# The experts' gelu written out with ScalarE's tanh, in a two-block model on one core

## The reference

```python
idx = ...
gate = jax.nn.softmax(best_s, axis=-1)
u = jnp.take(down, idx, axis=0)
act = jax.nn.gelu(jnp.einsum('thkd,td->thk', u, xb))
v = jnp.take(up, idx, axis=0)
return jnp.einsum('thk,thkd->td', (gate * act).astype(v.dtype), v)
```

## Time and profile before

| | |
|---|---|
| median of 3 runs | 3067.49 us (3066.1 to 3071.52) |
| the profiled execution | 3067.7 us |
| its span in the trace | 3065.5 us |
| layer 0 rows (first DMA issue to last diagonal) | 1703 to 2353 us |
| layer 1 rows | 2400 to 3053 us |
| busy over the span: PE, DVE, ACT, POOL | 88%, 69%, 43%, 19% |
| bytes moved by the row gathers | 536.9 MB |

### The profile page before, as it was taken

How to read it: one execution, slowest core, us unless ns; L and a number is a source line. 1 busy time by engine, 2 the same in 40 slices (tenths; PEclk the granted TensorE clock), 3 DMA queues, 4 the chain that set the end, 5 groups by cost and what they waited for, 6 DMA issues and landing times. The chain is left out here.

```text
span 3065.5 us, 45483 instructions
## 1 busy us (share of the span) xinstructions
PE 2693.6 (88%) x16982; PEld 1808.3 (59%) x16982; DVE 2114.3 (69%) x3898; ACT 1317.5 (43%) x2949; POOL 579.6 (19%) x516
## 2 busy tenths in 40 slices
PE   8999977999999987899989998877777899777777
PEld 6887776788788777778876653322223654223232
DVE  7756776775876677577555777777764777777764
ACT  5443444543544442454344344444443344444443
POOL 0000000000000000000000354444441244444442
PEclk9999999999999999899999999999999999999999
DMA  9855201785875510268643799999998699999997
GB/s 323 282 184 173 89 4 69 251 306 219 295 262 191 185 52 4 98 245 307 240 187 119 306 427 427 427 427 427 427 427 355 258 427 426 427 427 427 427 427 305
DMA packets 256748, 864.65 MB, mean 282 GB/s; under 512 B 15504, under 2 KB 139280, under 8 KB 183952
## 3 DMA queue, kind: packets, MB, share of 16 engines
q0 software_dynamic: 73728, 536.90, 41.6%
q1 hardware_dynamic: 182800, 324.85, 30.1%
HBM read 853.04 MB, written 8.65 MB: 281 GB/s over the span
## 5 line engine op out<-in xcount | busy, mean ns | idle before, releaser
L3634 POOL DMA_INDIRECT raw_weights<-peer_rows,expert_ids x208 | 232.2, 1116 | 2053.6 <-DVE expert_ids L152 1771.8
L3744 PE MATMUL banks<-raw_weights,diagonals 128*128 128x512 f32 x832 | 395.1, 615 | 92.2 <-ACT diagonals L185 92.2
L486 PE MATMUL banks<-weight_parts_hi,normedT_hi 128*128 128x512 f32 (+2 forms) x1152 | 452.8, 393 | 16.9 <-DVE weight_parts_lo L1662 5.4
L487 PE MATMUL banks<-weight_parts_lo,normedT_hi 128*128 128x512 f32 (+2 forms) x1152 | 441.4, 383 | 0.0
L488 PE MATMUL banks<-weight_parts_hi,normedT_lo 128*128 128x512 f32 (+2 forms) x1152 | 441.4, 383 | 0.0
L3744 PE MATMUL banks<-query_weights,diagonals 128*128 128x512 f32 x704 | 333.7, 611 | 70.1 <-ACT diagonals L185 69.6
L161 DVE CUSTOM_DVE_ANT_0 modulation<-raw_weights,normed 128x1024 f32<-128x1024 f32 x208 | 255.3, 1228 | 140.9 <-DMA raw_weights<-peer_rows,expert_ids 130.3
L3744 PEld LDWEIGHTS banks<-raw_weights,diagonals 128*128 128x128 f32 x832 | 151.7, 193 | 326.6 <-ACT diagonals L185 187.6
L185 ACT ACTIVATE gelu<-dots 128x1 f32<-128x1 f32 x512 | 102.3, 200 | 498.9 <-DVE dots L161 498.1
L3744 PE MATMUL banks<-modulation,diagonals 128*128 128x512 f32 x512 | 248.8, 622 | 63.8 <-ACT diagonals L185 63.7
L161 DVE CUSTOM_DVE_ANT_0 modulation<-query_weights,normed 128x1024 f32<-128x1024 f32 x176 | 216.0, 1227 | 113.2 <-DMA query_weights<-peer_rows,expert_ids 103.3
(11 more groups left out here) (407 smaller groups left out, 4495.3 us busy)
## 6 DMA issues: line engine op xcount, KB each, us to landing
raw_weights<-ffn_in SPq DMA_DIRECT2D x88, 1024.0 KB, 7.6
side_weights<-mod_tiles SPq DMA_DIRECT2D x48, 1024.0 KB, 5.9
raw_weights<-ffn_out SPq DMA_DIRECT2D x44, 1024.0 KB, 6.7
raw_weights<-w_in SPq DMA_DIRECT2D x28, 1024.0 KB, 5.0
query_weights<-peer_w_q SPq DMA_DIRECT2D x16, 1024.0 KB, 10.7
raw_weights<-w_in SPq DMA_DIRECT2D x10, 1536.0 KB, 6.5
raw_weights<-w_branch SPq DMA_DIRECT2D x8, 1024.0 KB, 7.3
raw_weights<-w_out SPq DMA_DIRECT2D x8, 1024.0 KB, 5.1
```

The source lines that it names most:

```text
L486: nc.tensor.matmul(out, lhs.hi, rhs.hi, start=start, stop=False)
L487: nc.tensor.matmul(out, lhs.hi, rhs.lo, start=False, stop=False)
L3634: nc.gpsimd.indirect_dma_start(out=ring.rows(g), out_offset=None, in_=table, in_offset=bass.IndirectOffsetOnAxis(ap=ids[:, n, t:t + 1], ax ...
L3744: last = nc.tensor.matmul(k.bank(2 * j + half), diag[:, g % DIAGS, :], ring.rows(g)[:, D + half * BANK:D + (half + 1) * BANK], start=t == ...
```

## The change

The gelu function of ScalarE is replaced by its formula. With x the dot product and w the gate weight halved, ScalarE computes x², w·x, GELU_CUBE·x² + GELU_ROOT, the tanh of that times x, and (tanh)·(w·x) + (w·x). The half is moved into `gate` on VectorE, as the second operation of an instruction that is there already. The first two copies are marked free, so they wait for no drain; the other three and the diagonal come after a drain each.

```diff
+GELU_ROOT = math.sqrt(2.0 / math.pi)
+GELU_CUBE = 0.044715 * GELU_ROOT
...
                 def gate(n):
                     dve.wait_ge(S["gate_exped"], n + 1)
                     o.recip(tot[:, n:n + 1], tot[:, n:n + 1])
-                    o.ts(best[:, n], best[:, n], tot[:, n:n + 1], ALU.mult).then_inc(S["gates_ready"], 1)
+                    o.ts(best[:, n], best[:, n], tot[:, n:n + 1], ALU.mult, 0.5, ALU.mult).then_inc(S["gates_ready"], 1)
...
                         act.wait_ge(S["dotted"], g + 1)
-                        o.fn(gelu[:, g:g + 1], dots[:, g:g + 1], ACT.Gelu_apprx_tanh, free=True)
-                        o.fn(coef[:, g:g + 1], gelu[:, g:g + 1], ACT.Copy, scale=best[:, n, t:t + 1])
+                        x = dots[:, g:g + 1]
+                        o.fn(gelu[:, g:g + 1], x, ACT.Copy, scale=x, free=True)
+                        o.fn(coef[:, g:g + 1], x, ACT.Copy, scale=best[:, n, t:t + 1], free=True)
+                        o.fn(gelu[:, g:g + 1], gelu[:, g:g + 1], ACT.Copy, scale=GELU_CUBE, bias=GELU_ROOT)
+                        o.fn(gelu[:, g:g + 1], gelu[:, g:g + 1], ACT.Tanh, scale=x)
+                        o.fn(gelu[:, g:g + 1], gelu[:, g:g + 1], ACT.Identity, scale=coef[:, g:g + 1], bias=coef[:, g:g + 1])
                         if g >= DIAGS:
 
                             act.wait_ge(S["prod"], g - DIAGS + 1)
-                        o.fn(diag[:, g % DIAGS, :], C("ident"), ACT.Copy, scale=coef[:, g:g + 1]).then_inc(S["grown"], 1)
+                        o.fn(diag[:, g % DIAGS, :], C("ident"), ACT.Copy, scale=gelu[:, g:g + 1]).then_inc(S["grown"], 1)
```

## The result

The changed kernel takes 3078.46 us (median of 6 runs, 3076.93 to 3086.31) against 3067.55 us for the kernel before (6 runs, 3066.1 to 3071.52). The ratio is 1.0034, with a 95% interval of 1.0019 to 1.0049: slower by 10.9 us. The profiled execution took 3077.13 us, its span 3075.0. Lines are numbered 2 higher behind the new constants (L187 is the helper of the earlier trace rows, L3750 the matmul of the earlier trace rows).

A forecast was written before the change was run, and what follows sets the result against it. DMA gathers bound the steady rows; in the rounds the longer ScalarE chain runs their queue dry. Idle DMA 1.1 to 2.6 and 0 to 1.4, ends 2.0, upper values plus 1: +7.0 us, 3074.5; range 3068.0 to 3088.0.

The forecast's parts named there:

- ScalarE's row: ScalarE per row: 1.63 us to the diagonal, 1.94 row to row, 1.01 longer than before; not the bound of steady rows.
- The loads: Two 1.28 us table loads around each `weigh` on ScalarE: taken as gone if Exp and Tanh share a table set.
- the loads stay: Rival: Tanh lies in another table set than Exp, so loads around each `weigh` remain; about +22 us, 3089.5; chance 0.10.
- The queue covers it: Rival: with a ScalarE step under about 1.88 us, gather-queue slack covers the rounds; only +2.0 us, 3069.7; chance 0.36.
- Faster, by the loads: Rival: removed loads, some 77 us of ScalarE, show as a gain; judged no gain (+1.7 us); chance 0.04 for faster.
- The round: From restart to restart at each layer's start: 17.82 us in place of 16.03, 18.15 with a `weigh`, against 17.19 of DMA.
- and the last takes 1.72: Term for the last of a round's seven rows on TensorE: 1.72 us, in the sum 2.35 + 9.70 + 1.72 = 13.77.
- The first burst: Layer 0's first seven rows, paced by ScalarE: 13.4 us against 12.0, less 0.27, so the first restart 1.1 late.
- The slack: Lateness the gather queue absorbs after the rounds: 6.0 to 7.5 us in layer 1, 8.2 to 9.7 in layer 0.
- If 7.0 is what a busy queue needs: Gather latency in a short queue, 7.0 us instead of the idle 5.5; layer 1's DMA idle time then 2.6, not 1.1.
- The ends: Last row of each layer, its chain exposed from landing to norm: 1.01 us longer each, 2.0 us in all.

The follow-up runs named there:

- e7: Changed kernel with the old gelu function in tanh's place, rest of the row unchanged, so the table loads stay: 3106.87 us, ratio 1.0121.
- e1: Changed kernel with ScalarE's copies of queriesT and key_scores two rows later, so three diagonals are ready at a restart: 3072.03 us, ratio 1.0015.
- e4: Kernel before with Tanh in place of the gelu function, rest of the formula left out: 3064.02 us, ratio 0.9986.
- e8: Kernel before with a spare gelu behind `weigh(0)`, loading its table ahead of the first row, and `weigh(1)` behind row 4: 3064.29 us, ratio 0.9994.
- e3: Changed kernel with the formula only in groups 4 to 15 of each layer, the gelu function in the others: 3070.12 us, ratio 1.0007.
- e2: Changed kernel with the formula only in groups 0 to 3 of each layer (64 rows), the old form in the others: 3072.51 us, ratio 1.0017.

## Why the prediction was right

The forecast was slower, 3074.5 us, +7.0 on the profiled execution; measured was +10.9, 3078.46, inside the range. The mechanism is the one that it named, a queue that runs short in the rounds and two exposed ends; its sizes were too small, and one loss of 1.6 us wasn't foreseen.

- **ScalarE's row: as predicted.** 1.93 from row to row and 1.63 to the diagonal, for 1.94 and 1.63. The second pointer costs 387 - 295 = 92 ns, for 88. ScalarE doesn't bind the steady rows: 330.2 of 463 us, and 427 GB/s.
- **The loads: gone, as taken.** Exp and Tanh share a set. The rival "the loads stay" falls with the 8 loads; its price of +22 was too low by e7.
- **"The queue covers it" falls.** The row is not under 1.88, and the DMA stands at 407 and 414 GB/s in the rounds of layers 1 and 0. e1, where the queue does cover it, shows what that rival would have been: +4.6 by its ratio (1.5 to 7.7), where it had 2.0.
- **"Faster, by the loads" falls for the change, but its premise was half wrong.** I had written that no row can come earlier with the DMA at 424 GB/s. The first rows of layer 0 can, by about 2 us (e4 and e8, row 72), for the queue is only filling there.
- **The round: a term too small.** Predicted 17.82, and 18.15 with a `weigh`; in layer 1 measured 18.06 to 18.34, and 18.25 to 18.54 with one. The step is "and the last takes 1.72": that row has waited for its diagonal, as the earlier trace rows already showed for another, and takes 1.98. That is 0.26 a round, 1.6 to 1.8 us per layer. That is all of the 1.6 that six rounds of layer 1 are over the forecast (109.53 for 107.9), and most of the 2.0 of layer 0 (127.77 for 125.7). How single rounds differ is in part "issue" time of ScalarE (8.5 us in the four groups above that show it, over all 512 rows).
- **The first burst: 1.1 us too much in layer 0.** I let ScalarE pace its first seven rows and took the first restart 1.1 later; it is 0.3 earlier (37.47 us after the first gather, for 37.80 in the second profile). In both of these traces TensorE ran its first rows at a lower clock (e4 above). In layer 1 it comes at 38.06 for 36.99, but e3, which has the old row there, has it at 40.01, so this difference shows nothing.
- **The slack: too large.** "If 7.0 is what a busy queue needs": the places where the DMA lost most show 8.98 and 9.65, with VectorE waiting and 297 GB/s. It isn't one number, though: the gather behind layer 1's restart before, issued at 2541.61, had its dot product at 2548.97, 7.4 later and with VectorE waiting too. In layer 1 11.5 - 6.0 = 5.5, of which 4.2 remain from row 104 on. In layer 0 the lateness of the rounds is 127.77 - 117.27 = 10.5, less 15.2 - 9.0 = 6.2: 4.3; the dot products are 3.6 late at row 72 and 3.0 at row 240. I had 1.4 and 2.6, and 1 for what followed: 5.0, for 7.1 by row 240.
- **The last rows of a layer: not foreseen.** Between row 240 and the last, 1.1 us more are lost in layer 0 and 0.5 in layer 1, single rows (242, 254) coming late by up to 0.7 us. e1 shows the same, e2 and e3 don't. So it is chance that 4.3, worked out for the rounds, is near the 4.1 by which layer 0's last dot product is late.
- **The ends: 2.0 predicted, and 2.0 shown for the chain.** Layer 1's is 1.0. Layer 0's is 50.6 us from the last dot product to the next gather for 48.8, 1.8. The other 0.8 stand in one group of matmuls in between. Chain of waits there, in the changed kernel and in the second profile of the kernel before:
```profile
2373.08 10.07 PE banks L3347 x32
...
2367.17 9.27 PE banks L3345 x32
```
Without this group the end takes 39.5 to 39.9 us in the five traces with the short row there and 40.5 in the five with the long one. The group itself takes 8.85 to 9.94 us in the former and 9.53 to 10.13 in the latter, so whether the change has a part in its 0.8 is open.

Summed by the table: 4.1 + 1.8 + 4.6 + 1.0 = 11.5 us, beside 10.9 between the medians (5.8 to 15.0). That is one pair of traces; the second trace of the changed kernel gives 13.4, so the sum can't be trusted to better than some 2 us.

Open: why TensorE stopped in the first profile of the kernel before; what scatters the start of layer 0's rows by some 10 us between runs, and whether the change has a part in it; what makes the last rows of a layer late; and why a gather issued to a short queue took 7.4 us in one place and 9.65 in the next.

## What to carry to other kernels

An engine that is 43% busy can still set the time at a restart, where a queue has to be filled and work goes hand to hand: price added instructions as a chain in each restart, not as a share of the stage. Cover is what a queue holds above the latency of a queue in work, which must be read where the queue has nearly run dry (here 7.4 to 9.65 us, not one figure), and from an execution without a disturbance. Where a kernel can't shorten a chain, it may help to let it run ahead: three diagonals in hand at the restart brought the first rounds back from 18.06 and 18.54 to 16.04 us, with all the added work still in them.

## What the runs showed of the hardware

- A gather queue that was nearly dry was slower than its idle latency suggests. Issue to dot product took 5.5 us when nothing else was under way, yet in two places the rate fell to 297 GB/s with 8.98 and 9.65 us between them, while the DMA engines' share was still 0.89.
- A row on TensorE that had waited for its diagonal took 1.98 to 2.00 us, one in a stream 1.72 (12.02 / 7), at a granted clock of 1.00 in both.
- After a wait of 2.60 us in the changed kernel, TensorE ran at a granted clock of 0.50 from 1728 to 1730, which is the 1.2 GHz level, and at 1.00 from 1732 on. After a wait of 1.60 us in e4 it stayed at 1.00; after 3.02 us in the kernel before it fell in one profile (16 matmuls in 8.75 us) and stayed at 1.00 in the other (7.13).
